# Chunk-causal attention regrouped: items of 64 queries and a pair of heads, stream items set between them, the scaling of the probabilities one item later on ScalarE

## What is computed

```python
def one_chunk(args):
    c, qb = args
    start = c * CHUNK
    kb = lax.dynamic_slice_in_dim(kp, start, band, axis=1)
    vb = lax.dynamic_slice_in_dim(vp, start, band, axis=1)
    valid = (start - BAND_PAST + offs_k) >= 0
    s = jnp.einsum('bqhd,bkhd->bhqk', qb, kb).astype(jnp.float32) * scale + bias[None]
    s = jnp.where(valid[None, None, None, :], s, NEG)
    p = jax.nn.softmax(s, axis=-1).astype(vb.dtype)
    return jnp.einsum('bhqk,bkhd->bqhd', p, vb)
```

## Time and profile before

| | |
|---|---|
| median of 3 runs | 3376.34 us (3374.62 to 3377.32) |
| span of the profiled execution | 3367.8 us; it was not timed by itself, and the median is 8.5 us more than its span |
| TensorE matmul busy | 3161.1 us (94%) |
| VectorE, ScalarE, GpSimd busy | 1456.8 (43%), 727.1 (22%), 96.9 us (3%) |
| mean granted TensorE clock | 0.954 of 2.4 GHz |
| attention, first score to first product of the output projection | 348.2 to 660.2 us of the span |

### The profile page before, as it was taken

The page is one execution under the profiler, slowest core; times in us unless marked ns, Lnnn a source line. Parts: engine busy times, 40 slices in busy tenths (PEclk is TensorE's granted clock), DMA queues, the critical chain, the costliest instruction groups (busy, mean ns, idle before and its releaser), DMA issues.

```text
span 3367.8 us, 45153 instructions
## 1 busy us (share of the span) xinstructions
PE 3161.1 (94%) x17988; PEld 3004.2 (89%) x17988; DVE 1456.8 (43%) x2451; ACT 727.1 (22%) x1160; POOL 96.9 (3%) x88
## 2 busy tenths in 40 slices
PE   6997989997999999999899999996979999999997
PEld 5996456797999999999799999996979999999996
DVE  6887333325333333333545455454352333333335
ACT  3121445513111111111311111220131111111111
POOL 3000000001000000000100000000010000000001
PEclk9998958998999999999899999996989999999998
DMA  3112410110111111110201111100201111111111
GB/s 120 45 44 70 153 41 1 69 44 32 45 41 41 44 44 44 44 39 32 94 33 39 39 40 39 40 33 21 100 26 56 38 39 45 44 39 44 38 44 57
DMA packets 47748, 163.11 MB, mean 48 GB/s; under 512 B 8416, under 2 KB 15888, under 8 KB 44768
## 3 DMA queue, kind: packets, MB, share of 16 engines
q1 hardware_dynamic: 42992, 148.45, 13.1%
q10 hardware_dynamic: 3456, 8.91, 0.7%
q0 software_dynamic: 1136, 3.27, 0.5%
HBM read 143.28 MB, written 18.92 MB: 48 GB/s over the span
## 4 chain that ended last, share of the span: by engine, by line
PE 89%; DVE 5%; issue 2%; ACT 2%; POOL 1%; DMA 1%; DVEq 0%; POOLq 0%; ACTq 0%; SPq 0%
PE PS L513 19%; PE PS L514 19%; PE PS L515 19%; PE PS L755 5%; PE PS L757 5%; PE PS L756 5%; PE PS L1406 4%; PE PS L1136 2%; PE PS L1167 2%; DVE HF L624 1%; PE PS L1149 1%; PE PS L1160 1%; PE PS L1118 1%; POOL SQ L425 1%; DVE HBL L634 1%
## 5 line engine op out<-in xcount | busy, mean ns | idle before, releaser
L513 PE MATMUL PS<-HAH,WH 128*128 128x384 f32 x1872 | 649.6, 347 | 27.0 <-issue 9.7
L514 PE MATMUL PS<-HAL,WH 128*128 128x384 f32 x1872 | 634.4, 339 | 0.0
L515 PE MATMUL PS<-HAH,WL 128*128 128x384 f32 x1872 | 633.8, 339 | 0.0
L513 PE MATMUL PS<-HBH,WH 128*128 128x384 f32 x1872 | 626.3, 335 | 0.0
L514 PE MATMUL PS<-HBL,WH 128*128 128x384 f32 x1872 | 626.2, 335 | 0.0
L515 PE MATMUL PS<-HBH,WL 128*128 128x384 f32 x1872 | 626.1, 334 | 0.0
L501 DVE TENSOR_TENSOR WL<-WR,WH 128x1024 fp32r<-128x1024 f32 x200 | 243.0, 1223 | 568.5 <-ACT WH L496 567.0
L513 PEld LDWEIGHTS PS<-HAH,WH 128*128 128x128 f32 x1872 | 358.4, 191 | 29.1 <-issue 19.9
L514 PEld LDWEIGHTS PS<-HAL,WH 128*128 128x128 f32 x1872 | 358.6, 192 | 9.7 <-issue 8.7
L755 PE MATMUL PS<-UH,WH 128*128 128x384 f32 x1056 | 360.3, 341 | 5.2 <-issue 5.0
L756 PE MATMUL PS<-UL,WH 128*128 128x384 f32 x1056 | 359.0, 340 | 0.0
(11 more groups left out here) (200 smaller groups left out, 2776.0 us busy)
## 6 DMA issues: line engine op xcount, KB each, us to landing
WR<-w_fi_in SPq DMA_DIRECT2D x88, 512.0 KB, 3.6
WR<-w_fo_in SPq DMA_DIRECT2D x44, 512.0 KB, 3.5
WR<-w_c_in SPq DMA_DIRECT2D x32, 512.0 KB, 4.2
WR<-w_ab_in SPq DMA_DIRECT2D x20, 512.0 KB, 3.6
CACHES<-k_cache_in SPq DMA_DIRECT2D x8, 1024.0 KB, 6.8
CACHES<-v_cache_in SPq DMA_DIRECT2D x8, 1024.0 KB, 5.0
X<-x_t_in SPq DMA_DIRECT2D x3, 1536.0 KB, 10.7
x_spill<-X SPq DMA_DIRECT2D x1, 4608.0 KB, 12.3
```

The lines of the kernel that those rows point to most:

```text
L513: nc.tensor.matmul(out, wh, hh(k, third(n)), start=(k == 0), stop=False)
L514: nc.tensor.matmul(out, wh, hl(k, third(n)), start=False, stop=False)
L515: mm = nc.tensor.matmul(out, wl, hh(k, third(n)), start=False, stop=(k == KT - 1))
```

## The change

The 64 prompt items become 16 chunks c x 4 head pairs f. An item's 128 rows are 2 heads x 64 queries. Its queries stand in a block-diagonal `QBD` (128x128 per pair, zeros beside the blocks), filled by 128 copies on GpSimd, so that scores contract over 128 rows and nothing has to be masked: the window is the chunk's own 576 keys (`window`), in 5 key tiles at most. The values of both heads are one product with 128 columns of weights; half of its output is not used. The first 8 chunks alternate with the 8 streams in rounds of 4 + 1 items. A stream's scores use the 32 rows of one head pair per product, written to 32 partitions each, and its values are 20 products of 32 columns of weights with 128 columns streamed in place of 5 of 128 with 512. Scores run two items ahead, and the scaling comes behind the next item's exponential. `PR` is split into `PRE`, `PRO` and `PRS` whose masked columns stay zero. Cut to its core:

```diff
+        ITEMS = NCK * PAIRS + NB
+        ROUND = PAIRS + 1
...
                     if b >= 2:
-                        sp.wait_ge(s_s, b - 1)
+                        sp.wait_ge(s_s, stream_item(b - 2) + 1)
                     sp.dma_start(KCA[:, b % 2], kc_d[b]).then_inc(s_kc[b % 2], 16)
...
+            pool.memset(QBD[:, :, :], 0.0).then_inc(s_qd, 1)
...
+            for c in range(NCK):
+                for f in range(PAIRS):
+                    i = c * PAIRS + f
+                    if c:
+                        pool.wait_ge(s_s, chunk_item(c - 1, f) + 1)
+                    for e in range(2):
+                        r = slice(CHK * e, CHK * (e + 1))
+                        pool.tensor_copy(QBD[r, f, r], X[r, f, c * CHK:(c + 1) * CHK]).then_inc(s_qd, 1)
...
+            t = c // 2
+            if c % 2 == 0:
+                return max(0, (4 - t) * P), CACHE + CHK
+            return ((4 - t) * P if t < 4 else CHK), CACHE + P
...
                     for f in range(AB):
-                        nc.tensor.matmul(score(s, slice(0, CACHE)), QB[:, s % 2, f, :], KCA[:, s % 2, f, :],
-                                         start=(f == 0), stop=(f == AB - 1))
+                        nc.tensor.matmul(score(s, 0, CACHE)[32 * f:32 * f + 32, :], QB[:, b % 2, f, :], KCA[:, b % 2, f, :],
+                                         start=True, stop=True)
...
-                    if cut:
-
-                        mm = nc.tensor.matmul(score(s, slice(0, 64)), late[:, :], plus[:, :], start=False, stop=True,
-                                              skip_group_check=True)
+                pe.wait_ge(s_qd, 1 + 2 * (c * PAIRS + f + 1))
+                lo, hi = window(s)
+                k0 = (c // 2 - 4) * P
+                for a, z in ((lo, CACHE), (CACHE, hi)):
+                    if a < z:
+                        mm = nc.tensor.matmul(score(s, a, z), QBD[:, f, :], X[:, AB + f, k0 + a:k0 + z], start=True, stop=True)
...
+                    for w in range(5):
+                        for f in range(AB):
+                            v = VCA[:, b % 2, w, tile(f)] if w < 4 else VTOK[:, NT - 1, tile(f)]
+                            mm = nc.tensor.matmul(PS[32 * f:32 * f + 32, out_bank(g), 0:P],
+                                                  PRT[:, s % 2, w * P + 32 * f:w * P + 32 * f + 32], v,
+                                                  start=(w == 0), stop=(w == 4))
...
-                for c in range(5 - nk, 5):
-                    mm = nc.tensor.matmul(PS[64 * (h % 2):64 * (h % 2) + 64, 6 + t % 2, tile(h // 2)],
-                                          VTOK[:, t - 4 + c, h * AD:(h + 1) * AD], PRT[:, s % 2, tile(c)],
-                                          start=(c == 5 - nk), stop=(c == 4))
+                for w in range(first_tile(s), 5):
+                    mm = nc.tensor.matmul(PS[:, out_bank(g), tile(f)], VTOK[:, c // 2 - 4 + w, tile(f)], PRT[:, s % 2, tile(w)],
+                                          start=(w == first_tile(s)), stop=(w == 4))
...
             scores(0)
+            scores(1)
             for s in range(ITEMS + 1):
-                if s + 1 < ITEMS:
-                    scores(s + 1)
+                if s + 2 < ITEMS:
+                    scores(s + 2)
+                if s < ITEMS:
+                    turn(s)
                 if s:
                     values(s - 1)
-                if s < ITEMS:
-                    turn(s)
...
                 if s < ITEMS:
                     probs(s)
                 if 1 <= s <= ITEMS:
+                    scaled(s - 1)
...
-                if s < ITEMS:
-                    scaled(s)
```

More of the change, by code:

```diff
@@ L55 @@
 EPS = 1e-6
-NEG = -1e30
+CHK = 64
+NCK = SEQ // CHK
+PAIRS = AH // 2
+BIASW = P + CHK
 LEVELS = 7
@@ L234, in encoder @@
         s_qb = sem("s_qb")
+        s_qd = sem("s_qd")
         s_s = sem("s_s")
@@ L1094, in ln_act, with group @@
                 T.add("hf")
-        ITEMS = NB + PT_TILES * AH
+        GROUPS = NCK + NB
         def item(s):
-            t, h = divmod(s - NB, AH)
-            return t, h, min(t + 1, 5)
-        def score(s, cols):
+            if s < NB * ROUND:
+                c, f = divmod(s, ROUND)
+                return (None, None, c) if f == PAIRS else (c, f, None)
+            c, f = divmod(s - NB * ROUND, PAIRS)
+            return c + NB, f, None
+        def group(chunk=None, stream=None):
+            if stream is not None:
+                return 2 * stream + 1
+            return 2 * chunk if chunk < NB else NB + chunk
@@ L1144, in turn @@
                 pe.wait_ge(s_pn, s + 1)
-                tiles = range(5 if s < NB else item(s)[2])
-                tiles = range(5 - len(tiles), 5)
                 need(pe, s_ptc, s)
-                for c in tiles:
-                    mm = nc.tensor.transpose(PSF[:, 2048 + c * P:2048 + (c + 1) * P], PR[:, s % 2, tile(c)], ident[:, :])
+                for w in range(first_tile(s), 5):
+                    mm = nc.tensor.transpose(PSF[:, 2048 + w * P:2048 + (w + 1) * P], probabilities(s)[:, tile(w)], ident[:, :])
@@ L1150, in turn @@
                 mm.then_inc(s_pt, 1)
             def values(s):
+                c, f, b = item(s)
                 pe.wait_ge(s_ptc, s + 1)
-                if s < NB:
-                    pe.wait_ge(s_vc[s % 2], 16 * (s // 2 + 1))
-                    need(pe, s_os, s)
-                    for c in range(5):
-                        v = VCA[:, s % 2, c, :] if c < 4 else VTOK[:, NT - 1, :]
-                        mm = nc.tensor.matmul(PS[:, 6, :], PRT[:, s % 2, tile(c)], v, start=(c == 0), stop=(c == 4))
+                if b is not None:
+                    g = group(stream=b)
+                    pe.wait_ge(s_vc[b % 2], 16 * (b // 2 + 1))
+                    need(pe, s_alo, 2 * (g - 1))
+                    for w in range(5):
[4 more added lines that the diff above has]
+                                                  start=(w == 0), stop=(w == 4))
@@ L1174, in stream_turn @@
                 pe.wait_ge(s_os, b + 1)
-                need(pe, s_alo, 2 * b)
-                for f in range(AB):
-                    mm = nc.tensor.transpose(PS[:, 7, tile(f)], OS[:, tile(f)], ident[:, :])
-                mm.then_inc(s_ot, 1)
+                nc.tensor.transpose(PS[:, out_bank(group(stream=b)), P:2 * P], OS[:, :], ident[:, :]).then_inc(s_ot, 1)
             pe.wait_ge(s_got["k"], N3 * AB)
```

258 lines of the change are left out of this document (135 added, 123 removed).

## The result

| | before | changed |
|---|---|---|
| median | 3375.48 us (3360.61 to 3377.32, 4 runs) | 3253.87 us (3251.78 to 3264.26, 4 runs) |
| ratio, 95% interval | | 0.9654 (0.9628 to 0.9681) |
| profiled execution, span | 3367.8 us | 3264.26 us, span 3262.5 us |
| attention ends (first product of the output projection) | 660.2 us | 553.4 us |
| the rest of the span behind it | 2707.6 us | 2709.1 us |

The change is 3.5% faster: 122 us by the two medians, some 117 by the ratio (0.0346 of 3375). By the two profiled executions it is 105 us, and the attention has them all: 106.8 us less until its end, 1.5 us more behind it.

What follows compares the result with a forecast made beforehand. TensorE, busy 94% of the span, was taken as the bound. The attention summed as 352.6 + 99 + 82 + 40 + 4.5 + 3.4 = 581.5 against 660.2 us, so span 3289, median 3298 us; range 3262 to 3338.

Steps and rivals of the forecast that it cites:

- first exponential: Start of the attention: ScalarE loads its table until 352.6 us and only then can run its first exponential.
- small items: The 32 items of query tiles t = 0 to 3: 82 us, between 64 with the clock up and 98 if not.
- streams: The 8 streams: 5 us each, 40 us in all, between 3.5 with strips side by side and 9.5 serial.
- full items: The 32 items with five key tiles: 3.1 us each, 99 us in all, with ends 2.95 and 3.3.
- ScalarE's ring: Per item: exponential, scaling, TensorE's transposes, copy, then the next exponential; 2.95 us in a full item.
- TensorE busy throughout: Sign for the full items: a period of 3.0 to 3.2 us between first transposes, with TensorE never idle.
- Rival 2: ScalarE's loop exceeds its parts; TensorE waits for the scaling, full items stay at 3.76 us; 3326 us, chance 0.07.
- rival 1: Column strips run one after another, streams take 76 us; 3319 us, or 3350 with small items at half clock; chance 0.20.
- Conv copies and end: Three convolution copies making TensorE wait 1.5 us each, 4.5 in all; 3.4 us more after the last exponential.
- At nothing: Work priced at no time: GpSimd's 128 copies, bias subtraction and memsets, streams' loads, VectorE's work, result rows.
- Rival 3: TensorE's clock stays at 1.2 GHz through the full items too, 5.6 us each; 31 us slower, 3408 us, chance 0.05.
- the low ends: Every attention term at its lowest, clock up throughout: attention ends at 542 us, 118 less, 3258 us.

Runs made afterwards that it cites:

- e6: The changed kernel with scores still two items ahead, but values before transposes and the scaling back in its own item; 3236.8 us, ratio 0.9625.
- e2: The changed kernel with the order of before: scores one item ahead, values before transposes, scaling in its own item; 3244.41 us, ratio 0.9649.
- e9: The changed kernel in its own order, with full items' values split into two halves of 64 columns; 3249.78 us, ratio 0.9658.
- e10: The changed kernel with extra unused products that keep TensorE busy ahead of the attention; 3265.37 us, ratio 0.97.
- e3: The changed kernel with the streams' products as before (128 columns of weights, four transposes); 3303.08 us, ratio 0.9814.
- e4: The kernel before with the column strips alone, streams still in a row at the front; 3322.69 us, ratio 0.9877.
- e5: The kernel before, unchanged, run again for a second profile; 3366.06 us, ratio 1.0004.
- e7: The changed kernel with the order of before and values as two halves of 64 columns of weights; 3241.47 us, ratio 0.9633.

## Why the prediction was off

The steps in the prediction's order, by the profile of the changed kernel:

| term | taken, us | measured, us |
|---|---|---|
| first exponential | 352.6 | 351.3 |
| from it to the first transposes | in the item | 1.0 |
| small items 82 and streams 40 | 122 | 102.7 |
| full items 99, conv copies 4.5, end 3.4 | 107 | 98.4 |
| end of the attention | 581.5 | 553.4 |
| rest of the span | 2707.6 | 2709.1 |
| median over the profiled span | +8.5 | -8.6 |

Two terms failed. The rounds (small items and streams) took 19 of the 28 us that the attention was overpriced by. And the median's place against the profiled span was taken as a fixed 8.5 us and missed by 17. Neither alone leaves the range: with the measured end of the attention and the prediction's own rest it would have been 3270 us, with the forecast end and the measured rest 3282.

- **Start: right.** The first exponential follows the table load, 1.3 us earlier because the part ahead was that much shorter in this execution.
- **Full items: the ring right, the limit named wrong.** ScalarE's ring was worked out as 2.95 us, and it is 2.95. I set 3.1 above it because I took TensorE's own work for 3.0 to 3.1; that is 2.72 to 2.83 (e6, e2). The step that failed is the sum from the earlier trace rows: transposes 0.70 stayed in it, and they take 0.54 with 128x128 products behind them (e2); scores came to 1.07 in place of 1.1 to 1.2. "TensorE busy throughout" was wrong too: it waits for the scaling in every item, which e9 shows to be the bound, and that the scaling ends last before the transposes was one of the prediction's own signs of being wrong. Rival 2 had the mechanism, with a size (3.76 us) that did not come.
- **Small items, "I take the middle, 82 us": this failed.** The middle stood between ScalarE's ring at full clock (64) and TensorE at half clock (98). With the streams at their two figures the ends were 92 and 146, and I took 122; measured 102.7. With the clock at 0.50 for only 10 us (e10) it is 98.5, so my low figure was some 4 to 7 us short. The hand-overs between ScalarE and TensorE in the small items (brackets of mostly 0.2 to 0.8 us before the transposes) are the likely reason, not tried alone. The lower clock cost 4 us by the runs and 7 at most by the estimate under e10, where the middle charged about 30. I knew from the earlier trace rows that light items had run at 0.50 for 90 us, and carried it over to a schedule in which TensorE does other work. The clock was at 0.50 for the first 19 us only, and in two stretches of 3.4 us. What in the regrouping keeps it up isn't shown: e3 shows that the strips are not needed, since its rounds were up with wide streams; e4 that they are not enough. The wider products of the items and the streams set between them are the candidates, and neither was tried alone.
- **Streams: between the bounds I leaned the wrong way.** 5 us each; at full clock the parts are 0.88 + 0.23 + 1.2 + 0.8, 3.1 us, below even my low end of 3.5. Nor have they a place of their own any more: a stream's item is 2.63 us from its transposes to the next item's (411.80 to 414.43) and the chunk item before it 2.40. The sixteen instructions of the earlier trace rows were the right row, and deserved their face value. Here 32 instructions of four column strips, all over 128 rows, take 1.08 us where one after another they would take 3.4: rival 1 falls. The prediction had drawn it from the Trainium skill's "TensorE: Matmul & The Clock Gate" (Part 3, The mechanism), by which weight loads overlap running matmuls only where the row group differs. That serial products follow from this was the prediction's own step: Part 3 of the same page (Measured speedup vs the span model) also gives three column strips of 512 columns as 2.38 times faster. And the rule itself isn't borne out: in e3 weight loads over all 128 rows (0.19 us each) lie beside products over all 128 rows that follow each other every 0.43 us. The Trainium skill's "TensorEngine Tiling (Array Packing)" (Key Properties) states a drain at a change of tiling; where the form changes from 128 to 32 columns of weights (414.90 in the changed kernel), TensorE's weight load stands idle for 0.17 us, which is the most that could be that drain there.
- **Conv copies and end: right in size.** Three items of 4.31 us in place of 2.95 and their followers at 3.0 to 3.3, some 5 us in all; 2.75 us from the last transposes to the projection.
- **At nothing: right.** GpSimd's two copies take 0.53 us (2.1 in three places, hidden; see below). Outside the attention the profile is 1.5 us longer, within what two profiles of one kernel differ by (7 us between the first profile of before and e5).
- **Rival 3 (slower at a low clock) fell**, as the clock stood at 1.00 through all full items.
- **The range.** The attention ended at 553.4 us, inside the prediction's own bounds of 542 and 617 and 11 us above the low end; the low ends did not all meet. They do move together, though: a clock that is up shortens small items and streams at once, so the two terms were not independent. Of the 44 us missed, 28 are the attention's. The other 16 are the median's place, 17 us, less the 1.5 us behind the attention: I added 8.5 us to the span, from the one profile of before, and the changed kernel's median lies 8.6 below its profiled span. Each timed run took 1.7 to 1.9 us more than its span, so of the 8.5 some 7 were the spread between executions and no cost. That the profiled execution of the changed kernel was the slowest of its four runs is chance.

## What to carry to other kernels

Where a stage ran at the low clock, and the change gives it other work, don't carry the clock over: work the sum out at full clock with every hand-over, price the low clock only by what TensorE does beyond its waits, and keep both corners in the range, since the terms move together. Don't carry one profiled execution's distance from the median over either: here it was +8.5 us for one kernel and -8.6 for the other. Narrow products (32 or 64 columns of weights) written to separate strips of the output can run side by side: four strips took under a third of the time of one wide product here, two halves 0.6 of it. A moved step is worth what the ring it opens or closes says; e2 and e9 read it off in one period of the timeline. Putting it back was worth 5 us of the attention, with scores two ahead and split values 17 by the ratios.

## What the runs showed of the hardware

- Four column strips over the full 128 rows of contraction overlapped: 8 instructions of 512 columns in 0.88 us from start to next group, against 3.44 with 128 columns of weights. Two halves of 64 columns overlapped in part: 20 instructions of 64 columns in 0.73 us, where 10 of 128 took 1.22 (e7, e2).
- Five transposes take 0.54 to 0.60 us from start to next where 128x128 products follow (e2, the changed kernel), 0.70 where 64-row products follow and 0.69 where products with 64 columns of weights follow (e9).
- GpSimd's pair of 64x64 copies, 0.53 us alone, took 2.13 us beside one operation of VectorE that reads and writes SBUF only, and 2.08 at the two other places of that operation. In the changed kernel's timeline:

```profile
460.92 0.53 POOL L513 COPY QBD<-X 64x64 f32<-64x64 f32 x2 [2.12 <-PE PS L1187]
...
469.79 1.76 DVE L1399 TENSOR_TENSOR HBL<-Y,HBH 128x1536 fp32r<-128x1536 f32 x1 [1.73 <-ACT HBH L1305]
469.80 2.13 POOL L513 COPY QBD<-X 64x64 f32<-64x64 f32 x2 [2.42 <-PE PS L1187]
```

  It hid, since a pair's queries are refilled four items before their use; in e2, with scores one item ahead, no wait of TensorE for it shows either (2.00 us at the most).
- TensorE's clock stood at 0.50 for 85 to 92 us in the kernel before and in e4, although matmuls counted as busy in 31.90 of 31.90 us at t = 2 and in 51.00 of 51.00 us of e4 (434 to 485 us), and at 1.00 in rounds 4 to 8 of the changed kernel with 56.90 of 64.80 us busy. In these rows the busy share alone doesn't tell the clock.
